# First attention of a two-block transformer: query tiles in the order 3, 2, 0, 1 instead of 3, 2, 1, 0

## What is computed

```python
def block_fn(args):
    qb, blk = args
    ...
    p_cmp = masked_softmax(jnp.einsum('bgrtd,bgnd->bgrtn', qb, kc_g), valid_c)
    o_cmp = jnp.einsum('bgrtn,bgnd->bgrtd', p_cmp, vc_g)
    ...
    o_slc = jnp.einsum('bgrtks,bgtksd->bgrtd', p_slc, vg)
    ...
    o_win = jnp.einsum('bgrts,bgsd->bgrtd', p_win, vwb)
    return o_cmp, o_slc, o_win
...
out = gates[:, :, 0] * to_bshd(o_cmp) + gates[:, :, 1] * to_bshd(o_slc) + gates[:, :, 2] * to_bshd(o_win)
...
mix = jnp.concatenate([y_ret, y_nsa], axis=-1).astype(x.dtype) @ w_out[l]
```

## Time and profile before

| | us |
|---|---|
| median of 3 runs | 2193.11 (2191.58 to 2193.16) |
| the profiled execution | 2191.74 |
| its span, from first to last instruction | 2190.0 |
| PE busy | 1977.3 |
| DVE busy | 1176.3 |
| ACT busy | 733.2 |
| mean granted clock of PE, share of full | 0.955 |

### The profile page before, as it was taken

How to read it: one execution, slowest core, us unless ns; L and a number is a source line. 1 busy time by engine, 2 the same in 40 slices (tenths; PEclk the granted TensorE clock), 3 DMA queues, 4 the chain that set the end, 5 groups by cost and what they waited for, 6 DMA issues and landing times.

```text
span 2190.0 us, 24671 instructions
## 1 busy us (share of the span) xinstructions
PE 1977.3 (90%) x8864; PEld 1568.7 (72%) x8864; DVE 1176.3 (54%) x1687; ACT 733.2 (33%) x1036; POOL 64.2 (3%) x63
## 2 busy tenths in 40 slices
PE   4897799889999987877799999996699999999997
PEld 3786577678888765665588888885466668888886
DVE  4566654575664667846554434455456635343444
ACT  3335222342332344323242323331334434232232
POOL 1020000200000020000000000000000000000000
PEclk9999799899999988998899999998799999999998
DMA  4224102222323331220023333332111112333333
GB/s 149 75 73 131 36 1 79 65 82 91 97 96 96 96 97 62 81 65 19 18 88 96 96 96 96 97 99 66 39 39 39 48 49 87 97 98 98 97 99 107
DMA packets 48325, 172.06 MB, mean 79 GB/s; under 512 B 5168, under 2 KB 5168, under 8 KB 48112
## 3 DMA queue, kind: packets, MB, share of 16 engines
q1 hardware_dynamic: 45504, 163.60, 24.0%
q10 hardware_dynamic: 2736, 7.32, 0.9%
HBM read 168.80 MB, written 2.10 MB: 78 GB/s over the span
## 4 chain that ended last, share of the span: by engine, by line
PE 31%; issue 17%; DVE 3%; ACT 1%; POOL 0%; POOLq 0%; ACTq 0%; DVEq 0%
PE ps L417 8%; PE ps L419 8%; PE ps L418 8%; PE ps L625 3%; PE ps L599 1%; PE ps L616 1%; DVE h_lo L1566 0%; PE ps L460 0%; ACT osbb L1198 0%; PE ps L477 0%; PE ps L634 0%; PE ps L856 0%; ACT w_hi L1004 0%; DVE w_lo L1479 0%; DVE y L1541 0%
## 5 line engine op out<-in xcount | busy, mean ns | idle before, releaser
L1004 ACT ACTIVATE w_hi<-raw 128x1024 fp32r<-128x1024 f32 x305 | 322.9, 1060 | 943.7 <-PE ps L419 942.9
L417 PE MATMUL ps<-h_hi,w_hi 128*128 128x512 f32 (+1 forms) x1376 | 552.9, 402 | 57.2 <-DVE w_lo L1479 35.4
L418 PE MATMUL ps<-h_lo,w_hi 128*128 128x512 f32 (+1 forms) x1376 | 542.1, 394 | 0.0
L419 PE MATMUL ps<-h_hi,w_lo 128*128 128x512 f32 (+1 forms) x1376 | 541.8, 394 | 0.0
L1479 DVE TENSOR_TENSOR w_lo<-raw,w_hi 128x1024 fp32r<-128x1024 f32 x305 | 373.3, 1226 | 216.1 <-ACT w_hi L1004 207.0
L417 PEld LDWEIGHTS ps<-h_hi,w_hi 128*128 128x128 f32 (+1 forms) x1376 | 262.1, 190 | 126.4 <-DVE w_lo L1479 35.6
L419 PEld LDWEIGHTS ps<-h_hi,w_lo 128*128 128x128 f32 (+1 forms) x1376 | 261.4, 190 | 56.8
L418 PEld LDWEIGHTS ps<-h_lo,w_hi 128*128 128x128 f32 (+1 forms) x1376 | 262.1, 190 | 55.8 <-issue 2.2
L417 PE MATMUL ps<-hid_hi,w_hi 128*128 128x512 f32 x688 | 268.6, 390 | 5.6 <-DVE hid_lo L1952 5.6
L418 PE MATMUL ps<-hid_lo,w_hi 128*128 128x512 f32 x688 | 268.4, 390 | 0.0
L419 PE MATMUL ps<-hid_hi,w_lo 128*128 128x512 f32 x688 | 268.3, 390 | 0.0
(11 more groups left out here) (347 smaller groups left out, 2296.7 us busy)
## 6 DMA issues: line engine op xcount, KB each, us to landing
raw<-in_panels SPq DMA_DIRECT2D x308, 512.0 KB, 3.6
x_in<-in_x ACTq DMA_DIRECT2D x1, 2048.0 KB, 16.7
x<-in_x ACTq DMA_DIRECT2D x1, 2048.0 KB, 8.6
out<-y SPq DMA_DIRECT2D x8, 256.0 KB, 2.1
first<-in_first ACTq DMA_DIRECT2D x1, 1568.0 KB, 19.9
second<-in_second ACTq DMA_DIRECT2D x1, 768.0 KB, 4.2
small<-in_small ACTq DMA_DIRECT2D x1, 332.0 KB, 5.2
masks<-in_masks ACTq DMA_DIRECT2D x1, 256.0 KB, 6.9
```

The costliest lines, as they stand in the source:

```text
L417: nc.tensor.matmul(out, a[0], b[0], start=start, stop=False)
L418: nc.tensor.matmul(out, a[0], b[1], start=False, stop=False)
L419: return nc.tensor.matmul(out, a[1], b[0], start=False, stop=stop)
L1004: nc.scalar.activation(w_hi[:, panel % 2, :], raw[:, panel % 4, :], ACT.Copy).then_inc(w_hi_ready, 1)
```

## The change

The tiles come in the order of a tuple, 3, 2, 0, 1, when the list of units is built, and the places to which turned tokens are written follow the same tuple. All else (rounds two units ahead, `rounds_at`, the loops) is unchanged code that reads the list. Lines of the changed kernel are 2 higher than those of before.

```diff
+
+NSA_ORDER = (3, 2, 0, 1)
...
     nsa = []
-    for qt in reversed(range(NT)):
+    for qt in NSA_ORDER:
         for g in range(2):
...
             act.wait_ge(token_turned, j + 1)
-            at = slice((NT - 1 - j) * P, (NT - j) * P)
+            at = slice(NSA_ORDER[j] * P, (NSA_ORDER[j] + 1) * P)
             nc.scalar.activation(h_hi[:, 4:8, at], ps[:, token_bank(j), :].rearrange("p (h q) -> p h q", h=4), ACT.Copy).then_inc(token_high, 1)
...
             dve.wait_ge(token_high, j + 1)
-            at = slice((NT - 1 - j) * P, (NT - j) * P)
+            at = slice(NSA_ORDER[j] * P, (NSA_ORDER[j] + 1) * P)
```

## The result

| | before | after |
|---|---|---|
| median, 12 runs each on the same chips | 2192.74 us (2190.99 to 2194.00) | 2199.11 us (2195.03 to 2202.03) |
| the profiled execution | 2191.74 | 2201.97 |
| mean granted clock of PE | 0.955 | 0.951 |

The ratio is 1.0029 with an interval of 1.0021 to 1.0036, so the change makes the kernel about 6.4 us slower. Each is taken against runs of before made beside it, whose medians were 2192.34 to 2192.74 us.) The forecast was +1.3 us, and the range ended at 2197.0: the prediction was wrong. The page of the kernel after answers to the earlier trace rows: PE has the same number of instructions and is busy 9.5 us longer.

What follows compares the result with a forecast made beforehand. TensorE, busy 90% of the span, was taken to bound the kernel, so reordering changes only waits: 1.0 + 0.7 - 0.4 = +1.3 us, forecast 2194.4 us against the median 2193.11, range 2191.2 to 2197.0.

Steps and rivals of the forecast that it cites:

- the bank wait: Units 4 and 5: the crowded turn's third round waits for a reduction to free its PSUM bank; 0.51 us each, together 1.0.
- VectorE's lateness into unit 5: Boundary into unit 5: `h_lo` queued behind three reductions in unit 4 starts the unit result 0.67 us late, once.
- The gain of 0.4 us from values directly behind scores: First attention, two head groups: values follow scores directly more often, which is cheaper than following rounds; 0.4 us less.
- The boundaries of 2.0 us: Between units, first score to first value matmul: 2.0 us whatever the next scores are; only unit 5's grows, to 2.7.
- the gap of 2.7 us: Behind the first attention's last unit: no matmul for 2.70 us; stays, being VectorE's chain, independent of the number of keys.
- rival (d): Unit boundaries: separating the short tile 0 units gains by spreading VectorE's waits, possibly passing the lower bound 2188.7 us; 2%.
- Rival (c): Units 4 to 5: idle waits drop the clock inside the stage for 14 us, costing 6.9 us, total 2201.3; 5%.
- Everything else moves with no price that I can find: Rest of the change: round sizes, token turning, last unit's bare work, the gap and x transfer cost nothing extra.
- rival (b): Behind the stage: the low-clock dip after the gap goes missing (2192.7 us) or lasts twice as long (2196.1); 18%.
- and so do all later ones: Behind the stage: all gaps after the 2.70 us one also come at another moment; no separate size given.
- Nothing in the order of tiles prefers one: Clock dip behind the gap: the order favours neither a missing dip (-0.4 us) nor a doubled one (+3.0).

Runs made afterwards that it cites:

- fill in units 1 to 4: Kernel before, with the scores of block 2 issued ahead of the values of block 0 in units 1 to 4 only: 2197.82 us, ratio 1.0016.
- the split kernel: Kernel after, crowded units' rounds 3 and 2 instead of 2 and 3, unit 4's `h_lo` ahead of turn 2's reductions, gap behind the attention filled: 2190.07 us, ratio 0.9993.

## Why the prediction was wrong

**The stage: right in kind and sum.** Units 4 and 5 each show the bank wait, 0.49 us against 0.51 in the forecast. Two terms were mis-sized, and they nearly cancel; that the sum came within 0.1 us is luck.

- VectorE's lateness into unit 5 was put at 0.67 us and measured at 0.38. The sum added full durations, and it had TensorE step into unit 5 at 1.30 us behind the third round, where it is 321.71 - 320.30 = 1.41. The rows show that a queued operation starts a little before the one ahead of it has ended by the profile: `h_lo` 0.61 us behind a reduction of 0.69, `negm` 0.60 behind an `h_lo` of 0.68, `w` 0.07 behind a `negm` of 0.16.
- A round was priced at 0.43 us by the row at 307.07. That row has the right shape but stands behind scores, and its first matmul is listed with 0.28 us. A round that stands behind values or behind another round begins with one of 0.36 and takes 0.49 to 0.54 in the traces: the earlier trace rows has 313.04 - 312.52 = 0.52, and after has 319.33 - 318.84 = 0.49 and 320.84 - 320.30 = 0.54. In the order of before three of the four rounds of this shape in a unit stood directly behind scores, in the new one none does. That is 0.22 us per unit, +0.44, which the sum did not have.
- The gain of 0.4 us from values directly behind scores came.

Measured terms: 0.98 + 0.38 + 0.44 - 0.4 = +1.40, and the stage shows +1.42; forecast +1.3. The boundaries of 2.0 us and the gap of 2.7 us stayed as forecast. Of rival (d), the gain by spreading, nothing was seen.

**Rival (c) did not happen.** The crowded units kept a granted clock of 1.00, as the earlier trace rows had suggested. The Trainium skill, "TensorE: Matmul & The Clock Gate", section "A second HAM failure mode: psum-queue depth-cycling", describes cycling through PSUM banks as something that can make the clock swing; with a bank wait of 0.49 us in each, neither crowded unit shows that.

**The step that failed is "Everything else moves with no price that I can find"**, with rival (b) as its only allowance. Rival (b) named the right mechanism, gaps that come at another moment, and sized it at one low stretch: 1.7 us more or less. That one stretch did what it said (349 us: 3.4 lost instead of 1.7, and the traces of after with nine more matmuls and with only `h_lo` moved show that it can also stay short). But "and so do all later ones" stood in the same paragraph, and no price followed from it. What the runs show in its place is 9.0 us more of lost clock in the profiled execution, only 1.7 of it in that stretch, and about 5 of the 6.4 us between the medians. The trace of before shows 21 stretches at low clock with 98.6 us of lost time. A forecast that took the list as movable would have needed a range of some ±8 us for this edit, as the neutral delay of the same size costs 8.2; ±1.7 came from a single row. The 6 us of rival (c) were in the text, but tied to the wrong place.

**"Nothing in the order of tiles prefers one"** holds in its words: the same +1.4 us without the order gives 2200.95, and the order with 2.1 us more gives 2196.62. It was wrong as a reason for a small price, since for the actual shift, +1.4 us, the long list is not an even chance. By their times (2195.5 or more once the stage's 1.4 us are taken off) 9 of 12 runs of after had it, and none of the 12 runs of before. Of the 121 runs of before in the later comparisons, two, at 2198.7 and 2198.9, may have had it.

**What is shown and what isn't.** Shown: the loss is in the low-clock stretches behind the stage; a neutral delay of the same size at the same place brings it in the old order; a further delay, or the filled gap, takes it away in the new one; the same delay at 555, 906 or 1137 us leaves the median alone. Not shown by an experiment: that the place of the work against the clock's steps, which sorts the traces, is the cause. Not shown at all: by what rule the chip goes from one list to the other, and how a delay at the end of the attention moves that place. The long stretch at 349 us is not the key, since the kernels with the moved `h_lo` and with fill in units 1 to 4 have a long list with 1.7 us there. Nor is the filled gap a sure cure: three of eleven runs of before with the gap filled, and two of eleven of the split kernel, were 4 to 7 us above their kernel's median, whereas after with it had none. The first place where the lists part is the gap ahead of 817 us (820 in after).

## What to carry to other kernels

Price a reordering by its waits, and then look at what its length does to everything behind: where the trace has many stretches at low clock, a shift of 1 us can cost 5 us or more (here +1.0, +1.4 and -0.9 us did) or be given back (here at 555 us), and that belongs into the range of the forecast. To judge an edit of that size, run a neutral delay of the same size at the same place beside it, and the edit with a further delay; otherwise the order gets the blame for the moment. The gain that lasted here came from leaving TensorE less idle time: the filled gap together with the filled boundaries won 6.0 us, and every one of the eight runs was below the fastest of before.

## What the runs showed of the hardware

The length of a TensorE-bound stretch and the time of the program are not monotone in each other: before, +0.7, +1.4, +2.0 and +3.4 us of the same matmuls gave medians of 2192.7, 2196.0, 2201.0, 2194.2 and 2195.8 us (before itself was 2192.3 to 2192.7 in the comparisons). Shortening it by 0.9 us from unit 2 on gave 2197.8. A stretch of low clock appears 470 us behind the place of the delay, at 820 us, in work that ran at full clock before (16 matmuls in 5 us at clock 1.00, against 12 at 0.66). The same matmul can start within 0.2 us of the same moment of the program, behind a gap of the same 1.81 us, and meet full clock in one kernel and low clock in another. And one program can fall in two groups from run to run, up to 10 us apart: the nine extra matmuls gave 2191.3 to 2195.2 seven times and 2201.0 to 2204.1 four times, so a median of few runs of such a kernel says little.
